# One expert turn with all 128 tokens of the busiest expert, its partner in a half turn, and pairs read from a table

## The chip, the cores and the metric

The kernel runs on one core of a Trainium2 chip. A core has a matmul engine (TensorE, PE in the profile, with its weight loads as PEld), a vector engine (VectorE, DVE), a scalar engine (ScalarE, ACT), GpSimd (POOL) and a sync engine (SyncE, SP) that issues most of the DMAs here. The metric is the device time of one execution in microseconds, as the median of three runs.

## The reference, cut to what matters

The program is one transformer block over 256 tokens of width 1024 with a mixture of experts in it, followed by two further layers. Only the mixture of experts is changed. Each token picks 4 of 32 experts, and each expert is two matrix products with a gated activation between them:

```
def moe_ffn(h, router_w, router_b, w1, b1, w2, b2):
    ...
    logits = (xt @ router_w + router_b).astype(jnp.float32)
    top_v, top_e = lax.top_k(logits, TOP_K)          # TOP_K = 4 of 32
    gate = jax.nn.softmax(top_v, axis=-1)
    ...
    def expert_block(args):
        rows, e = args
        xb = xt[rows]
        hb = xb @ w1[e] + b1[e]                       # 1024 -> 2048
        g, u = hb[:, :D_EXPERT], hb[:, D_EXPERT:]
        g = jnp.minimum(g, SWIGLU_LIMIT)
        u = jnp.clip(u, -SWIGLU_LIMIT, SWIGLU_LIMIT)
        glu = g * jax.nn.sigmoid(g * SWIGLU_ALPHA)
        return ((u + 1.0) * glu) @ w2[e] + b2[e]      # 1024 -> 1024
    ...
    out = jnp.zeros((N, D), y.dtype).at[row_tok].add(y * row_w[:, None].astype(y.dtype))
```

The weights of one expert are 1024 x 2048 and 1024 x 1024 in fp32, 12 MB together, and all 32 experts are used. With the reference's inputs its router sends 69 tokens to expert 9, 63 to expert 6 and fewer to every other; expert 8, the other one of expert 9's pair, gets 27.

## The kernel before

The mixture of experts is a row of 17 turns, named in `MOE_TURNS` (L123): pair 0, then "over", then pairs 1 to 15. A pair turn does experts 2q and 2q+1 together. Each expert has CAP = 64 token places, and the two experts lie side by side on the two 64-column strips of the PE array. The "over" turn is for the one expert that has more than 64 tokens. It takes that expert's tokens 64 to 127, and both strips work on the same 64 tokens: one strip multiplies the even 128-row chunks of the weights and the other the odd ones (`rows_gemm` L1861, `c.over`). `turn_rows` L1883 then adds the two strips by a matmul with `twin`, which folds them, where a pair turn has a transpose. The weights of that expert are so loaded twice, once in its own pair turn and once in the "over" turn.

A turn has three parts, gate, up and down. In each, a pair turn uses 8 slots, a slot being 128 x 2048 fp32 (1 MB, two 128-row chunks of one expert's weights). The "over" turn uses 4 slots in each part. For a pair turn a slot costs 4 matmuls of 128x64 by 512 columns, and so does a slot of the "over" turn. Each matmul stands twice in the trace, since fp32 takes two passes, so 32 records are 16 matmuls.

The order on PE in a turn is (`experts` L1860): the first half of the gate part, the result of the turn before (L1911, 16 records; after the "over" turn ahead of it the biases, L1925), the second half of gate, the selection transposed (L1900), a piece of another network (`ctx_products(0)`, L1956, from turn 2 on), the first half of up, the gate transposed (L1892, or L1890 with `twin` in the "over" turn), the second half of up, half of the gather of the next turn's tokens (L1849), the transposed up part, the other half of the gather, `ctx_products(1)`, and the down part. Turns 0 and 1 have no context pieces, but two `mod` slots each (L2206 on DVE). In turns 13 to 16 the context piece is another one (L1967).

All these weights stream through a ring of 10 places: places 0 to 8 and the buffer hT (`MOE_RING` L120). SP walks one list (`stream` L926): for each transfer it waits until PE has released the place's holder of 10 transfers before, and issues the next. Which expert is the busiest is found at run time by DVE (`find_busiest` L2656), which leaves its number in `route_ints` and then posts `count_ready`; SP and DVE read it into a register (`busiest_expert` L918, TENSOR_LOAD L921) for the "over" turn. Addresses of all other turns are constants. If an expert other than the busiest has more than 64 tokens, or the busiest more than 128, a further loop of rounds runs; here it does not.

Of the kernel before, what the change touches and what calls it, by code (L numbers as in the profile page):

```python
# [63 lines left out]
COLS_E = N_EXPERTS + 2  # L64
# [58 lines left out]
MOE_TURNS = [0, "over"] + list(range(1, PAIRS))  # L123
MOE_COLUMNS = [PAIRS * 2 if pair == "over" else 2 * pair for pair in MOE_TURNS]
# [24 lines left out]
class Plan:  # L149
# [59 lines left out]
    def moe_slot(self, n, pair, j):  # L209

        name, e, at = MOE_SLOTS[j]
        self.moe_slots[n, j] = s = len(self.stream)
        self.stream.append((name, pair if pair == "over" else 2 * pair + e, at, 2, 0, D))
        return s
# [6 lines left out]
    def moe_part(self, n, pair, part, kps):  # L221

        for kp in kps:
            for e in range(1 if pair == "over" else 2):
                s = self.moe_slot(n, pair, part * PART_SLOTS + 2 * kp + e)
                if kp < DC // 2 - 1 or (e == 0 and pair != "over"):
                    self.slot_signal(s)
# [324 lines left out]
def build(nc, ins, out):  # L552
    with ExitStack() as ctx:
# [29 lines left out]
        route_ints = sb("route_ints", [P, 4], I32)  # L583
# [88 lines left out]
        place2 = small[:, 512:512 + TB * COLS_E].rearrange("p (b e) -> p b e", b=TB)  # L672
        gate2 = small[:, 580:580 + TB * COLS_E].rearrange("p (b e) -> p b e", b=TB)
        busiest = small[:, 648:648 + N_EXPERTS]
# [113 lines left out]
        def source(entry, busiest=None):  # L788
            name, index, k0, rows, c0, cols = entry
            if name in ("exp_w1", "exp_w2"):  # L790
                return ins[name][busiest if index == "over" else index][k0].rearrange("p (k n) -> p k n", k=2)
# [12 lines left out]
        class First:  # L804
# [3 lines left out]
            def __init__(self, n, busiest=None):  # L808
                pair = MOE_TURNS[n]
                self.n, self.turn, self.over, self.last = n, n, pair == "over", n + 1 == len(MOE_TURNS)  # L810
                self.experts = (busiest, busiest) if self.over else (2 * pair, 2 * pair + 1)
                self.columns_next = None if self.last else MOE_COLUMNS[n + 1]
# [27 lines left out]
        class Later:  # L840

            x, over = "_x", False
# [75 lines left out]
        def busiest_expert(eng):  # L918

            eng.wait_ge(sem("count_ready"), 1)  # L920
            return eng.value_load(route_ints[0:1, 1:2], min_val=0, max_val=N_EXPERTS - 1)  # L921
# [3 lines left out]
        def _(sp):  # L925
            def stream(s0, s1, busiest=None):  # L926
                for s in range(s0, s1):
# [3 lines left out]
                    sp.dma_start(slot_ap(s, entry[3], entry[5]), source(entry, busiest)).then_inc(landed[PLAN.place[s]], 16)  # L931
# [6 lines left out]
            over = MOE_TURNS.index("over")  # L938
            stream(behind, PLAN.moe_slots[over, 0])
# [2224 lines left out]
```

## Time and profile before

| what | value |
|---|---|
| time, median of three runs (lowest, highest) | 2520.53 us (2520.11, 2523.71) |
| the profiled execution's own time | 2523.49 us |
| its span from the first to the last instruction | 2521.4 us |
| PE busy in the span | 2468.8 us (98%) |
| DMA moved | 778.13 MB, mean 309 GB/s |
| the expert weights among it | 396 transfers of 1 MB |

The span lies 2.1 us below the profiled execution's own time. The mixture of experts runs from about 374 us to about 1482 us of the span. The page cuts the span into 40 slices of 63 us, so that it covers slices 7 to 23 and parts of those beside them. The lines of instructions and of waits say where an engine stood idle and what ended that; the timeline gives single stretches with their start.

### The profile page before, as it was taken

How to read it: one execution, taken by the hardware profiler on the slowest of the kernel's cores; microseconds unless marked ns; L12 is line 12 of the kernel's file. 1: busy time of each engine (PE TensorE's matmuls, PEld its weight loads, DVE VectorE, ACT ScalarE, POOL GpSimd, SP SyncE). 2: the span in 40 equal slices, each digit the busy share in tenths (PEclk: the TensorE clock that was granted, in tenths of full speed). 3: DMA queues.
4: the chain of work that ended last, by engine and by line, in shares of the span. 5: the costliest groups of instructions: out<-in, count | busy, mean ns of one | idle time of the engine just before them, and what ended most of it. 6: DMA issues, size and time to landing. Idle time of an engine off the chain costs nothing. (4 is left out here: it accounts for less than half of the span.)

```text
span 2521.4 us, 36563 instructions
## 1 busy us (share of the span) xinstructions
PE 2468.8 (98%) x16110; PEld 1897.8 (75%) x16110; DVE 1170.8 (46%) x1547; ACT 732.2 (29%) x896; POOL 0.4 (0%) x6
## 2 busy tenths in 40 slices
PE   7999999999999999999999999999999999999998
PEld 6898884555555555555555569999899999999998
DVE  6778763211111111111111149976477667777563
ACT  3355331111011111110111033444544344344442
POOL 0000000000000000000000000000000000000000
PEclk9999989999999999999999999999999999999999
DMA  9844568999999999999999967778267757865651
GB/s 394 302 166 151 218 252 356 421 400 417 418 418 418 419 418 418 418 418 417 397 417 400 397 234 268 282 260 275 74 221 287 288 210 287 305 241 210 215 188 51
DMA packets 156801, 778.13 MB, mean 309 GB/s; under 512 B 12353, under 2 KB 38081, under 8 KB 90593
## 3 DMA queue, kind: packets, MB, share of 16 engines
q1 hardware_dynamic: 152304, 768.68, 78.0%
q10 hardware_dynamic: 4336, 7.07, 0.9%
q8 instruction: 129, 2.11, 0.3%
q14 instruction: 32, 0.25, 0.0%
HBM read 774.66 MB, written 1.05 MB: 308 GB/s over the span
## 5 line engine op out<-in xcount | busy, mean ns | idle before, releaser
L1874 PE MATMUL psum<-ring,arena 128*64 128x512 f32 x2864 | 694.8, 597 | 6.4 <-DMA ring<-in_exp_w 3.5
L1874 PEld LDWEIGHTS psum<-ring,arena 128*64 128x64 f32 x2864 | 220.5, 137 | 418.8 <-issue 415.4
L1491 PE MATMUL psum<-h_high,w_low 128*128 128x256 f32 x1728 | 490.0, 284 | 0.0
L1491 PE MATMUL psum<-h_high,w_high 128*128 128x256 f32 x1728 | 484.3, 281 | 1.4 <-ACT h_high L1290 1.2
L1491 PE MATMUL psum<-h_low,w_high 128*128 128x256 f32 x1728 | 483.6, 281 | 0.0
L2847 DVE TENSOR_TENSOR w_low<-ring,w_high 128x2048 fp32r<-128x2048 f32 (+1 forms) x172 | 374.5, 2191 | 204.2 <-ACT w_high L1277 203.5
L1277 ACT ACTIVATE w_high<-ring 128x2048 fp32r<-128x2048 f32 (+1 forms) x172 | 313.7, 1835 | 380.0 <-PE psum L1491 297.6
L1491 PEld LDWEIGHTS psum<-h_high,w_high 128*128 128x128 f32 x1728 | 328.2, 190 | 5.0 <-issue 4.2
L1491 PEld LDWEIGHTS psum<-h_low,w_high 128*128 128x128 f32 x1728 | 324.7, 188 | 0.0
L1491 PEld LDWEIGHTS psum<-h_high,w_low 128*128 128x128 f32 x1728 | 324.6, 188 | 0.0
L1191 ACT ACTIVATE arena<-psum 128x1024 f32<-128x1024 f32 x68 | 56.8, 862 | 557.5 <-PE psum L1874 557.5
L2206 DVE SCALAR_TENSOR_TENSOR ring<-ring,cond_rows 128x1024 f32<-128x1024 f32 x174 | 206.6, 1220 | 15.3 <-ACT cond_rows L1006 14.5
L2771 DVE TENSOR_TENSOR arena<-psum,arena 128x1024 f32<-128x1024 f32 x32 | 39.2, 1225 | 375.9 <-PE psum L1911 375.9
L1491 PE MATMUL psum<-m_low,w_high 128*128 128x256 f32 x704 | 197.2, 280 | 0.0
L1491 PE MATMUL psum<-m_high,w_high 128*128 128x256 f32 x704 | 196.4, 279 | 0.7 <-DVE arena L2884 0.7
L1491 PE MATMUL psum<-m_high,w_low 128*128 128x256 f32 x704 | 196.8, 280 | 0.0
L2741 DVE TENSOR_TENSOR arena<-psum,vecs 128x512 f32<-128x512 f32 x68 | 43.8, 686 | 296.9 <-PE psum L1892 288.0
L1956 PE MATMUL psum<-arena,ring 128*128 128x256 f32 x640 | 141.4, 379 | 0.0
L1874 PE MATMUL psum<-hT,arena 128*64 128x512 f32 x304 | 134.2, 595 | 0.0
L1491 PEld LDWEIGHTS psum<-m_high,w_high 128*128 128x128 f32 x704 | 132.3, 188 | 0.9 <-DVE arena L2884 0.9
L1491 PEld LDWEIGHTS psum<-m_high,w_low 128*128 128x128 f32 x704 | 132.3, 188 | 0.0
L1491 PEld LDWEIGHTS psum<-m_low,w_high 128*128 128x128 f32 x704 | 132.2, 188 | 0.0
(348 smaller groups left out, 2975.5 us busy)
## 6 DMA issues: line engine op xcount, KB each, us to landing
ring<-in_exp_w SPq DMA_DIRECT2D x358, 1024.0 KB, 11.6
ring<-in_ffn_w SPq DMA_DIRECT2D x108, 1024.0 KB, 5.7
ring<-in_mod_w SPq DMA_DIRECT2D x95, 1024.0 KB, 6.8
hT<-in_exp_w SPq DMA_DIRECT2D x38, 1024.0 KB, 11.7
ring<-in_w_in SPq DMA_DIRECT2D x24, 1024.0 KB, 8.5
ring<-in_ffn_w SPq DMA_DIRECT2D x32, 768.0 KB, 4.9
ring<-in_ctx_w SPq DMA_DIRECT2D x20, 1024.0 KB, 11.8
ring<-in_even_w_in SPq DMA_DIRECT2D x12, 1024.0 KB, 8.1
```

Source lines behind the costliest of these rows:

```text
L1191: act.activation(moe_buf(dst)[:, 0:cols], c.unit(name)[:, 0:cols], ACT.Copy, scale=scale).then_inc(c.free(name), 1)
L1277: act.activation(high_ap(m, cols), slot_ap(s, 2, cols), ACT.Copy).then_inc(sem("w_high_ready"), 1)
L1491: return pe.matmul(unit(u0 + j // 4)[:, (j % 4) * T:(j % 4 + 1) * T], w[:, k % 2, j * P:(j + 1) * P], h[:, k, :], start=first, stop=stop, ...
L1874: mm = pe.matmul(u[strip, cols], x[:, k, strip], c.slot(of)[:, row, cols], start=(kp == 0 and (c.over or r == 0)), stop=(kp == DC // 2 - 1 ...
L1956: mm = pe.matmul(u[:, a * T:(a + 1) * T], w[:, k, a, :], ctx_h[:, k, :], start=(k == 0 and a == 0), stop=(k == DC - 1), skip_group_check=True)
L2206: last = dve.scalar_tensor_tensor(to, w[:, j, :], 1.0, cond_rows[:, row, :], ALU.mult, ALU.mult, accum_out=sums)
L2741: last = dve.tensor_tensor(dst[:, :, strip], rows[:, :, strip], wide(bias, CAP), ALU.add)
L2771: dve.tensor_tensor(dst, c.unit(name).rearrange("p (k t) -> p k t", k=4), dst, ALU.add).then_inc(c.free(name), 1)
L2847: dve.tensor_tensor(low_ap(s, cols), slot_ap(s, 2, cols), high_ap(m, cols).bitcast(F32), ALU.subtract).then_inc(sem("w_split"), 1)
```

## The change

The turns become pair 0, "busiest", "partner" and 14 more pair turns, again 17. In "busiest" both strips take the same expert, strip 0 its tokens 0 to 63 and strip 1 its tokens 64 to 127, from the same slots; so a slot there costs 8 matmuls in place of 4. The other expert of that pair, the partner, takes a turn of its own in the way of the old "over" turn, with its even and odd chunks on the two strips. The pairs of the 14 later turns are read from a table of 16 numbers that DVE writes: entry q is q, or 1 where q is the busiest expert's pair. Pair 0 is left out of the search for the busiest expert, since its turn is already under way. The expert of every turn from turn 1 on is now a number in a register, on SP for the addresses, on DVE for the biases and the selection, on ACT for the gates.

```
-MOE_TURNS = [0, "over"] + list(range(1, PAIRS))
-MOE_COLUMNS = [PAIRS * 2 if pair == "over" else 2 * pair for pair in MOE_TURNS]
+MOE_TURNS = [0, "busiest", "partner"] + list(range(2, PAIRS))
+TURN_COLUMNS = {"busiest": N_EXPERTS, "partner": N_EXPERTS + 2}
+BUSIEST_AT, PARTNER_AT, PAIRS_AT = 1, 2, 4
...
-            for e in range(1 if pair == "over" else 2):
+            for e in range(1 if pair in TURN_COLUMNS else 2):
                 s = self.moe_slot(n, pair, part * PART_SLOTS + 2 * kp + e)
...
+        def turn_of(eng, n):
+
+            kind = MOE_TURNS[n]
+            if kind == 0:
+                return 0
+            at, most = {"busiest": (BUSIEST_AT, N_EXPERTS - 1), "partner": (PARTNER_AT, N_EXPERTS - 1)}.get(
+                kind, (PAIRS_AT, PAIRS - 1))
+            at += 0 if kind in TURN_COLUMNS else kind
+            return eng.value_load(route_ints[0:1, at:at + 1], min_val=0, max_val=most)
...
-            stream(behind, PLAN.moe_slots[over, 0])
-            stream(PLAN.moe_slots[over, 0], PLAN.moe_slots[over + 1, 0], busiest_expert(sp))
-            stream(PLAN.moe_slots[over + 1, 0], PLAN.moe_end)
+            stream(behind, PLAN.moe_slots[1, 0], (0, 1))
+            sp.wait_ge(sem("count_ready"), 1)
+            for n in first_turns[1:]:
+                end = PLAN.moe_end if n + 1 == len(MOE_TURNS) else PLAN.moe_slots[n + 1, 0]
+                stream(PLAN.moe_slots[n, 0], end, First(n, turn_of(sp, n)).experts)
...
             for n in first_turns:
-                experts(First(n))
+                pair_next = n + 1 < len(MOE_TURNS) and MOE_TURNS[n + 1] not in TURN_COLUMNS
+                experts(First(n, None, turn_of(act, n + 1) if pair_next else None))
...
-                        slots = [part * PART_SLOTS + 2 * kp + e for e in range(1 if c.over else 2)]
+                        slots = [part * PART_SLOTS + 2 * kp + e for e in range(1 if c.over or c.alone else 2)]
...
-                                    row, of = (e, slots[0]) if c.over else (r, slots[e])
+                                    row, of = (e, slots[0]) if c.over else (r, slots[0 if c.alone else e])
...
+            partner, pairs = small[:, 160:160 + E], small[:, 392:392 + PAIRS]
...
                 link(dve.scalar_tensor_tensor(key, counts, float(E), iota, ALU.mult, ALU.subtract))
+                link(dve.memset(key[:, 0:2], -1e6))
                 link(dve.max(key_top, key))
...
+                of_pair, other_of_pair = [a.rearrange("p (q e) -> p q e", e=2) for a in (busiest, partner)]
+                for e in range(2):
+                    last = dve.tensor_copy(other_of_pair[:, :, e], of_pair[:, :, 1 - e])
+                link(last)
+                link(dve.tensor_tensor(key, partner, iota, ALU.mult))
+                link(dve.tensor_reduce(small[:, 457:458], key, AX_X, ALU.add))
+                link(dve.tensor_copy(route_ints[:, PARTNER_AT:PARTNER_AT + 1], small[:, 457:458]))
+                link(dve.tensor_reduce(pairs, of_pair, AX_X, ALU.add))
+                link(dve.scalar_tensor_tensor(pairs, iota[:, 0:PAIRS], -1.0, pairs, ALU.add, ALU.mult))
+                link(dve.tensor_tensor(pairs, iota[:, 0:PAIRS], pairs, ALU.subtract))
+                link(dve.tensor_copy(route_ints[:, PAIRS_AT:PAIRS_AT + PAIRS], pairs))
                 dve.tensor_copy(route_ints[:, 0:1], small[:, 460:461]).then_inc(sem("count_ready"), 1)
...
+            of = 0
             for n in first_turns:
-                experts(First(n, busiest_expert(dve) if MOE_TURNS[n] == "over" else None), steps)
+                of_next = turn_of(dve, n + 1) if n + 1 < len(MOE_TURNS) else None
+                experts(First(n, of, of_next), steps)
+                of = of_next
```

On PE, in turn 1 of the kernel before, from the result of turn 0 to the first gather (L1911 is that result, L1874 the weight products, L1900 the selection, L1890 the transposed gate with `twin`, L1849 the gather; here a row is matmuls, not records):

```order
L1911 MATMUL psum<-arena 128x256 x8
L1874 MATMUL psum<-ring,arena 64x512 x4
L1874 MATMUL psum<-hT,arena 64x512 x4
L1900 MATMUL psum<-consts,arena 128x128 x2
L1874 MATMUL psum<-ring,arena 64x512 x8
L1890 MATMUL psum<-arena 128x128 x8
L1874 MATMUL psum<-ring,arena 64x512 x8
L1849 MATMUL psum<-arena 128x128 x8
```

The same place in the changed kernel (its lines stand 15 further down; L1907 is the plain transposed gate):

```order
L1926 MATMUL psum<-arena 128x256 x8
L1889 MATMUL psum<-ring,arena 64x512 x8
L1889 MATMUL psum<-hT,arena 64x512 x8
L1915 MATMUL psum<-consts,arena 128x128 x2
L1889 MATMUL psum<-ring,arena 64x512 x16
L1907 MATMUL psum<-consts,arena 128x128 x8
L1889 MATMUL psum<-ring,arena 64x512 x16
L1864 MATMUL psum<-arena 128x128 x8
```

Between the same neighbours each part of turn 1 has twice the products, on the same number of slots.

On SP, the issues of turn 2 and the start of turn 3 in the kernel before (in_ctx_w are the context's weights):

```order
L931 DMA ring<-in_exp_w 128x2048 x8
L931 DMA ring<-in_ctx_w 128x2048
L931 DMA hT<-in_exp_w 128x2048
L931 DMA ring<-in_exp_w 128x2048 x7
L931 DMA ring<-in_ctx_w 128x2048
```

The end of turn 2 and the start of turn 3 in the changed kernel (TENSOR_LOAD reads the turn's number from `route_ints`, ISA rows are register arithmetic):

```order
L944 ISA
L944 DMA ring<-in_exp_w 128x2048
L934 TENSOR_LOAD route_ints
L934 ISA x2
L944 ISA
L944 DMA ring<-in_exp_w 128x2048
L944 ISA
L944 DMA ring<-in_exp_w 128x2048
```

A load now stands ahead of each turn's first transfer, and a register instruction ahead of each expert transfer.

On DVE, the end of the search for the busiest expert in the kernel before; the last row posts `count_ready`:

```order
L2663 TENSOR_REDUCE small<-small 128x1
L2664 TENSOR_TENSOR small<-small,consts 128x32
L2665 TENSOR_REDUCE small<-small 128x1
L2666 CAST route_ints<-small 128x1
L2667 CAST route_ints<-small 128x1
```

The same place in the changed kernel, from the first of the two casts to the last:

```order
L2684 CAST route_ints<-small 128x1
L2687 COPY small<-small 128x16 x2
L2689 TENSOR_TENSOR small<-small,consts 128x32
L2690 TENSOR_REDUCE small<-small 128x1
L2691 CAST route_ints<-small 128x1
L2692 TENSOR_REDUCE small<-small 128x16
L2693 SCALAR_TENSOR_TENSOR small<-consts,small 128x16
L2694 TENSOR_TENSOR small<-consts,small 128x16
L2695 CAST route_ints<-small 128x16
L2696 CAST route_ints<-small 128x1
```

Nine small instructions stand between the two casts, and a memset (L2676) ahead of them.

## Rows read from the trace of the kernel before

**Rows 1.** The page's 40 slices of the span: granted clock in tenths, and GB/s

```profile
PEclk9999989999999999999999999999999999999999
GB/s 394 302 166 151 218 252 356 421 400 417 418 418 418 419 418 418 418 418 417 397 417 400 397 234 268 282 260 275 74 221 287 288 210 287 305 241 210 215 188 51
```

**Rows 2.** Waits of PE, 300 to 1500 us: total us, times, longest

```profile
PE psum L1892 <- ACT arena L1191: 5.7, 2, 4.5
PE psum L1874 <- DMA ring<-in_exp_w: 3.5, 2, 3.0
```

**Rows 3.** Timeline of ACT: start, us; a turn's finished gate part taken from PSUM

```profile
562.11 1.30 ACT L1191 ACTIVATE arena<-psum 128x1024 f32<-128x1024 f32 x2 [16.42 <-PE psum L1874]
627.42 1.30 ACT L1191 ACTIVATE arena<-psum 128x1024 f32<-128x1024 f32 x2 [16.42 <-PE psum L1874]
...
1285.66 1.30 ACT L1191 ACTIVATE arena<-psum 128x1024 f32<-128x1024 f32 x2 [16.42 <-PE psum L1874]
...
1356.15 1.30 ACT L1191 ACTIVATE arena<-psum 128x1024 f32<-128x1024 f32 x2 [16.42 <-PE psum L1874]
```

**Rows 4.** Windows: us, then busy of the engines; last granted clock, DMA share, GB/s

```profile
420.00:444.00 24.00, 23.48 (x108) 9.48 (x104) 4.04 (x6) 1.11 (x2) 0.00 (x0) 1.00 1.01 422
448.00:450.00 2.00, 2.00 (x6) 0.53 (x4) 1.97 (x5) 0.00 (x0) 0.00 (x0) 0.50 1.03 430
484.00:486.00 2.00, 2.00 (x5) 1.17 (x5) 0.00 (x0) 0.00 (x0) 0.00 (x0) 0.50 1.03 430
562.00:627.00 65.00, 65.00 (x324) 33.83 (x322) 8.89 (x13) 7.22 (x13) 0.00 (x0) 1.00 1.01 418
1285.00:1356.00 71.00, 71.00 (x350) 38.42 (x346) 8.05 (x11) 7.23 (x13) 0.00 (x0) 1.00 0.98 398
```

**Rows 5.** Timeline of PE, turns 1 and 2: start, us, [idle before <- what ended it]

```profile
434.93 1.94 PE L1874 MATMUL psum<-ring,arena 128*64 128x512 f32 x8 [0.52 <-DMA ring<-in_exp_w]
436.79 3.72 PE L1911 MATMUL psum<-arena 128*128 128x256 f32 x16
...
447.45 6.50 PE L1874 MATMUL psum<-ring,arena 128*64 128x512 f32 x16 [2.98 <-DMA ring<-in_exp_w]
453.88 2.05 PE L1890 MATMUL psum<-arena 128*128 128x128 f32 x16
455.86 3.65 PE L1874 MATMUL psum<-ring,arena 128*64 128x512 f32 x16
...
463.12 1.95 PE L1849 MATMUL psum<-arena 128*128 128x128 f32 x16
466.82 5.37 PE L1874 MATMUL psum<-ring,arena 128*64 128x512 f32 x24 [1.75 <-issue]
...
484.70 5.01 PE L1911 MATMUL psum<-arena 128*128 128x256 f32 x16
...
496.94 7.07 PE L1956 MATMUL psum<-arena,ring 128*128 128x256 f32 x32
```

**Rows 6.** Timeline of PEld in turn 1, a weight load that waited for a slot

```profile
450.04 0.27 PEld L1874 LDWEIGHTS psum<-ring,arena 128*64 128x64 f32 x2 [0.59 <-DMA ring<-in_exp_w]
```

**Rows 7.** SP by source line (ns min/median/max), its waits in turns 3 on, DMA landing

```profile
L921 SPq TENSOR_LOAD <-route_ints x1: 471/471/471, 412.4 to 412.4; - x1
...
L931 SPq FUSED_REGOPS  x12: 37/37/48, 413.2 to 444.1; - x12
...
SPq L931 <- PE psum L1956: 164.5, 19, 10.7
...
ring<-in_exp_w SPq DMA_DIRECT2D x358, 1024.0 KB, 11.6
```

**Rows 8.** Timeline around the search: DVE's last casts, its next work, PE's first product

```profile
367.29 0.15 DVE L2667 CAST route_ints<-small 128x1 int32<-128x1 f32 x1
...
373.71 0.49 DVE L2686 TENSOR_TENSOR arena<-consts,small 128x128 f32<-128x128 f32 x2 [3.97 <-ACT arena L1185]
...
373.73 13.95 PE L1874 MATMUL psum<-ring,arena 128*64 128x512 f32 x64 [1.11 <-ACT arena L1185]
```

More of the change, by code:

```diff
@@ L212, in moe_slot @@
         self.moe_slots[n, j] = s = len(self.stream)
-        self.stream.append((name, pair if pair == "over" else 2 * pair + e, at, 2, 0, D))
+        self.stream.append((name, (n, e), at, 2, 0, D))
         return s
@@ L223, in moe_part @@
         for kp in kps:
-            for e in range(1 if pair == "over" else 2):
+            for e in range(1 if pair in TURN_COLUMNS else 2):
                 s = self.moe_slot(n, pair, part * PART_SLOTS + 2 * kp + e)
-                if kp < DC // 2 - 1 or (e == 0 and pair != "over"):
+                if kp < DC // 2 - 1 or (e == 0 and pair not in TURN_COLUMNS):
                     self.slot_signal(s)
@@ L806, in build, with __init__ @@
             x = ""
[L808 to L812, printed above, removed]
+            def __init__(self, n, of=None, of_next=None):
+                kind = MOE_TURNS[n]
+                self.n, self.turn, self.last = n, n, n + 1 == len(MOE_TURNS)
+                self.alone, self.over = kind == "busiest", kind == "partner"
+                self.experts, self.columns_next = None, None
+                if of is not None:
+                    self.experts = (of, of) if kind in TURN_COLUMNS else (of * 2, of * 2 + 1)
+                if not self.last and MOE_TURNS[n + 1] in TURN_COLUMNS:
+                    self.columns_next = TURN_COLUMNS[MOE_TURNS[n + 1]]
+                elif of_next is not None:
+                    self.columns_next = of_next * 2
                 self.gathers = n
@@ L840, in build @@
         class Later:
-            x, over = "_x", False
+            x, over, alone = "_x", False, False
             def __init__(self, r, i, last):
@@ L916, in many, with stream @@
             return eng.value_load(route_ints[0:1, 0:1], min_val=0, max_val=T)
-        def busiest_expert(eng):
-            eng.wait_ge(sem("count_ready"), 1)
-            return eng.value_load(route_ints[0:1, 1:2], min_val=0, max_val=N_EXPERTS - 1)
+        def turn_of(eng, n):
+            kind = MOE_TURNS[n]
+            if kind == 0:
[4 more added lines that the diff above has]
+            return eng.value_load(route_ints[0:1, at:at + 1], min_val=0, max_val=most)
         @block.sync
         def _(sp):
-            def stream(s0, s1, busiest=None):
+            def stream(s0, s1, experts=None):
                 for s in range(s0, s1):
@@ L1876, in rows_gemm @@
                                                    stop=(kp == DC // 2 - 1 and (c.over or r == 1)), skip_group_check=True)
-                                    if half == 1 and row == 1:
+                                    if half == 1 and row == 1 and (e == 1 or not c.alone):
                                         if kp == DC // 2 - 1 and e == 1:
@@ L2665, in find_busiest @@
                 link(dve.tensor_reduce(small[:, 462:463], key, AX_X, ALU.add))
-                link(dve.tensor_copy(route_ints[:, 1:2], small[:, 462:463]))
-                dve.tensor_copy(route_ints[:, 0:1], small[:, 460:461]).then_inc(sem("count_ready"), 1)
-                both = busiest[:, None, :].broadcast_to([P, TB, E])
-                for of in (place2, gate2):
-                    link(dve.tensor_tensor(tmp2, both, of[:, :, 0:E], ALU.mult))
-                    link(dve.tensor_reduce(of[:, :, E], tmp2, AX_X, ALU.add))
@@ new lines, in find_busiest @@
+                link(dve.tensor_copy(route_ints[:, PAIRS_AT:PAIRS_AT + PAIRS], pairs))
+                dve.tensor_copy(route_ints[:, 0:1], small[:, 460:461]).then_inc(sem("count_ready"), 1)
+                for one, at in ((busiest, E), (partner, E + 2)):
+                    both = one[:, None, :].broadcast_to([P, TB, E])
+                    for of in (place2, gate2):
+                        link(dve.tensor_tensor(tmp2, both, of[:, :, 0:E], ALU.mult))
+                        link(dve.tensor_reduce(of[:, :, at], tmp2, AX_X, ALU.add))
+                        link(dve.tensor_copy(of[:, :, at + 1], of[:, :, at]))
```

27 lines of the change are left out of this document (13 added, 14 removed).

## The prediction

> **What bounds the kernel now.** I read the slices first: over the mixture of experts the DMAs move 397 to 421 GB/s and the clock is near full all along [rows 1]. So both the weight stream and PE are candidates, and the question decides the case, because the change leaves out one loading of an expert (12 transfers of 1 MB) and leaves PE's products as they are. The waits of PE come next. Over 300 to 1500 us PE stood idle for expert weights 3.5 us in all, in two pieces [rows 2]; the 5.7 us for ACT lie in turn 0 for the greater part, which the change leaves alone. Then the length of a pair turn: 65.31 us (562.11 to 627.42) with the first context piece, 70.49 us (1285.66 to 1356.15) with the second, longer one [rows 3]. In the first kind of turn 26 transfers of 1024 KB are 27.26 MB in 65.31 us, 417 GB/s, as the window says (418); in the longer turn the rate falls to 398 while PE is busy for all of it [rows 4]. A stream that bounded the turn would hold its rate. With 422 GB/s shown where PE waited on it, the stream needs 64.6 us for 27.26 MB, 0.7 us less than the turn takes. So the pair turns are bounded by PE, with the DMAs close behind.
>
> The Trainium skill, in Trainium Kernel Development and Optimization, section Performance Expectations, calls matmul busy time a poor measure of the distance to the limit, since matmuls are pipelined. That speaks against reading anything from PE's 98%, and nothing here is read from it.
>
> The only place where the stream comes last is turn 1, the "over" turn. It spends 4 matmuls on a slot, 1.8 to 1.9 us (8 records), and pauses only for transposes, while a slot needs 1.049 MB / 422 GB/s = 2.49 us to arrive. The ring runs empty. PE waits 0.52 us for the second gate slot, 2.98 us for the first up slot, and once more inside the next 16 records, where a weight load of the second up slot waits for its DMA [rows 5, 6]. These 16 records take 6.50 us where 16 equal ones soon after take 3.65, and the clock there is at 0.50, 1.2 of 2.4 GHz, after the 2.98 us of idling [rows 4, 5].
>
> **The change part by part.** PE: the products of turns 0 to 2 were full, half, full and become full, full, half. The folding transposes, the biases and the two context pieces occur as often as before. Sum: 0.
>
> Stream: turn 1 still takes 12 expert slots and 2 mod slots, in the same ring places, but now spends 8 matmuls on a slot, about 3.6 us for 16 records [rows 5], against the 2.49 us that a slot needs to arrive. The second gate slot lands at 434.93. PE had done with the first at 434.41 and, with 3.6 us a slot in place of 1.8, now does so at about 436.2. The first up slot lands at 447.45 and was wanted at 444.47; the gate part before it grows by 4 x 1.8 us less the 0.52, so it is wanted at about 451. The second lands at 450.04 and is wanted at about 454.7. So each arrives 1 to 4 us early, the slack grows by 1.1 us a slot, and all three waits go: 0.52 + 2.98 + (6.50 - 3.65) = **6.35 us**. What is late next? After the transposed up part, PE fills in a gather and then waits for DVE's hidden part: from 463.12 to 466.82, 1.75 us idle [rows 5]. Turn 1 still has no context piece there, so that stays as it is. Turn 2, now the half turn, has two context pieces to spread its 12 slots, about 14.7 MB (35 us of stream), over some 43 us of PE: 65.31 less the 96 records that it has fewer, at 3.65 for 16. It starts with a full ring. The turns after it are the pair turns of before, where PE waited for no slot with a poorer start [rows 2]. So the stream gives nothing further back and takes nothing.
>
> The slow clock after the biases (a result of 5.01 us in place of 3.72 [rows 5], clock 0.50 [rows 4]) moves with the half turn from turn 2 to turn 3. I keep it; if it vanished, 1.29 us more would be won.
>
> SP: each turn from 1 on begins with a register load, 0.47 us, and each expert transfer has a register instruction of 0.037 us [rows 7], 24 of them 0.9 us in a turn. The kernel before does both in its "over" turn. I cost them at nothing: SP waits for releases most of a turn, the longest wait on a context piece being 10.7 us, and by the ring's order it comes right behind a turn's first transfer, so right behind the load. A transfer lands 11.6 us after its issue, which at 2.49 us each is some four others ahead of it [rows 7]; a delay of half a microsecond in the issue is lost in that queue. Without the cover it costs what rival 3 says.
>
> ACT and DVE: a load a turn, and a register instruction by each bias, selection and gate operation. The load took 0.47 us on SP [rows 7], and I take it to be the same here. Both stand in front of waits that dwarf it: ACT idles 16.42 us ahead of the gate's eviction [rows 3]. DVE's bias steps lie in the chain to the hidden part, some 0.1 us longer, hidden by a 7 us context piece [rows 5] in all turns but 0 and 1. So 0 to 0.2 us in all; I take 0.
>
> The search: ten small DVE instructions ahead of `count_ready`, each like the cast at 0.15 us and somewhat over with its link, 2 to 2.5 us. `count_ready` moves from about 367.5 to about 370; PE's first product starts at 373.73, when ACT has the gathered tokens, which doesn't depend on it [rows 8]. The rest of the table work (about 1.5 us) delays DVE's next selection from 373.7 to about 375; ACT wants that only after turn 0's gate part, 14 us later [rows 8]. Cost 0. If that cover were gone the whole would be 4 us, once.
>
> Behind the mixture the ring is entered at another place, since 12 transfers are gone. The first two transfers of the next network may go out some microseconds earlier; that network starts from a chain of sums and norms, not from them. I take 0, bounds 0 and -1 us.
>
> Sum: -6.35 us. The profiled execution's 2523.49 becomes 2517.1; the median of the runs lies 3.0 us below that execution, and the same step from it gives 2520.53 - 6.35 = **2514.2 us**.
>
> **The rivals.** (1) The stream bounds after all. Then the 12 transfers count in full, 12.58 MB / 418 GB/s = 30.1 us: 2490.4 us. For it: the DMA share of 1.01 in every pair turn. Against: no wait of PE on a slot after turn 1, and the lower rate in the longer turns [rows 2, 4]. The Trainium skill, DMA: Bandwidth & Descriptors, section Specifications, gives about 358 GB/s as what HBM serves to one core and 435 GB/s as the fabric's ceiling. By the first, as an estimate, a pair turn would be 76 us of stream and this rival would hold; the trace's 418 to 422 GB/s disagrees with it and lies under the second, by which a turn's stream would be an estimated 62.7 us.
>
> (2) The wait moves and takes the clock with it: the idle stretch before turn 1's down part, or a slot that still comes late, drops PE to 1.2 GHz for one stretch as at 448 us. That costs the 2.85 us of that stretch: 2520.53 - 6.35 + 2.85 = 2517.0 us, no change by the bound below. For it: idling of 2.98 us was followed by the low level. Against: the same 1.75 us of idling before down is followed by 24 records in 5.37 us, full speed [rows 5].
>
> (3) Slower: SP's own work. If each of the 14 later pair turns showed its whole load and register work, 0.47 + 0.9 = 1.4 us, as a hole in the stream, and PE ran into that hole, the cost is 14 x 1.4 = 19 us: 2533 us. It decides from 6.35 / 14 = 0.45 us a turn on. For it: the stream has only 0.7 us of room in a turn, and the instructions are in every turn. Against: the depth of the queue, above.
>
> (4) It doesn't do what it says: if the busiest expert were in pair 0, or another had over 64 tokens, the rounds would run, 16 further pair turns of 65 us and more. The reference's counts (expert 9 with 69, the next 63) exclude that but for rounding.
>
> (5) The clock stays up after the biases: 7.6 us won, 2512.9 us.
>
> **How the numbers follow.** Forecast 0.66, rival (1) 0.04, (2) 0.16, (3) 0.07, (4) 0.01, (5) 0.06. About 0.2%, 5 us, is what a measurement of this kernel can tell from no change. The forecast lies only 1.3 us beyond that, and the three runs of before spread over 3.6 us, so about a seventh of it falls within. Faster: 0.57 + 0.04 + 0.06, about 0.66; within 0.26; slower 0.08. The range takes in the forecast, (2) and (5), with about 2 us of spread: 2510.5 to 2519.5 us.
>
> **What would show it.** Right: no wait of PE on an expert slot in turn 1 and none later; a full clock from 420 us on until the biases, now in turn 3; the first context piece of turn 3 some 6.4 us earlier than before; pair turns still 65.3 and 70.5 us, with the DMA rate at 418 and 398; 12 fewer expert transfers. Wrong: pair turns shorter than 65 us (then the stream bounded, rival 1), pair turns longer, with PE waiting for slots near a turn's start (rival 3), or a new stretch at half clock in turns 1 to 3 (rival 2).

## The result

The changed kernel takes 2526.02 us (median of 12 runs, 2520.83 to 2528.15) against 2520.88 us of the kernel before on the same chip (12 runs, 2515.11 to 2523.71): a ratio of 1.0020 with a 95% interval of 1.0011 to 1.0029. It is 5.1 us slower where 6.3 us less were forecast, and lies above the predicted range. The execution that was profiled took 2525.25 us, with a span of 2523.4 us.

| us of the span, one profiled execution each | before | changed | difference |
|---|---|---|---|
| first expert product | 373.73 | 370.51 | -3.22 |
| from there to the last result of the mixture | 1104.53 | 1099.09 | -5.44 |
| from there to the first product of the next network | 21.04 | 27.24 | +6.20 |
| from there to the end | 1022.1 | 1026.6 | +4.5 |

In this pair of executions the mixture so gained nearly what was forecast (the means of all traces, further down, say 4.0 us). The loss is behind it, in code that the change doesn't touch. The four rows add up to 2.0 us and not 5.1: the first one is spread from execution to execution, as the last table shows. In the changed kernel PE's lines stand 15 further on, ACT's 14: L1889 was L1874, L1579 was L1564 (the products that keep the clock up), L1506 was L1491 (the products of the later networks).

PE's waits of the changed kernel from 300 to 1500 us (total us, times, longest), beside [rows 2]:

```profile
PE psum L1907 <- ACT arena L1205: 5.7, 2, 4.5
PE psum L1579 <- issue: 4.3, 1, 4.3
...
PE psum L1889 <- DMA ring<-in_exp_w: 1.2, 1, 1.2
```

The wait for expert weights fell from 3.5 to 1.2 us, and what is left lies ahead of turn 1, in the down part of turn 0. The second row is new: 4.3 us in one piece that the profile ties to nothing. ACT's timeline, a turn's finished gate part, beside [rows 3]:

```profile
553.45 1.30 ACT L1205 ACTIVATE arena<-psum 128x1024 f32<-128x1024 f32 x2 [21.78 <-PE psum L1889]
618.76 1.30 ACT L1205 ACTIVATE arena<-psum 128x1024 f32<-128x1024 f32 x2 [16.42 <-PE psum L1889]
...
1277.00 1.30 ACT L1205 ACTIVATE arena<-psum 128x1024 f32<-128x1024 f32 x2 [16.42 <-PE psum L1889]
...
1347.48 1.30 ACT L1205 ACTIVATE arena<-psum 128x1024 f32<-128x1024 f32 x2 [16.42 <-PE psum L1889]
```

Each row comes 8.66 us earlier (the last 8.67) than its fellow in [rows 3], at the start of the pair turns as at their end, and the turns are as long as they were, 65.31 and 70.48 us. Windows of the changed kernel (busy times of the engines; granted clock, DMA share and GB/s last), beside [rows 4]:

```profile
448.00:450.00 2.00, 2.00 (x12) 0.83 (x12) 1.97 (x5) 1.79 (x5) 0.00 (x0) 1.00 1.05 426
619.00:684.00 65.00, 65.00 (x322) 33.56 (x321) 8.99 (x13) 6.98 (x13) 0.00 (x0) 1.00 1.01 418
1277.00:1347.00 70.00, 70.00 (x346) 38.28 (x345) 8.05 (x11) 7.22 (x13) 0.00 (x0) 1.00 0.98 398
1476.00:1481.00 5.00, 0.73 (x2) 0.43 (x3) 2.90 (x2) 4.98 (x4) 0.00 (x0) 0.56 0.53 215
1481.00:1485.00 4.00, 4.00 (x10) 3.19 (x11) 1.59 (x1) 0.10 (x1) 0.00 (x0) 0.50 0.02 4
```

Turn 1 has the full clock now, and the DMA rates are the old ones, 418 and 398 GB/s. The last two rows are the place of the loss: PE all but idle, and then at half clock.

**The first loss: a pause behind the mixture.** Timelines of PE around the second norm, in the kernel before and in the changed one (start, us, idle before and what ended it):

```profile
1478.26 3.72 PE L1911 MATMUL psum<-arena 128*128 128x256 f32 x16 [1.15 <-ACT arena L1191]
1484.59 3.39 PE L1564 MATMUL psum<-consts 128*128 128x256 f32 x8 [2.60 <-PEq L1569]
...
1494.72 4.05 PE L1564 MATMUL psum<-consts 128*128 128x256 f32 x18
```

```profile
1469.60 3.72 PE L1926 MATMUL psum<-arena 128*128 128x256 f32 x16 [1.15 <-ACT arena L1205]
1476.01 0.48 PE L1579 MATMUL psum<-consts 128*128 128x256 f32 x1 [2.70 <-PEq L1584]
1480.75 3.36 PE L1579 MATMUL psum<-consts 128*128 128x256 f32 x7 [4.26 <-issue]
1483.90 1.06 PE L1600 MATMUL psum<-hT,consts 128*128 128x256 f32 x2
...
1492.26 4.05 PE L1579 MATMUL psum<-consts 128*128 128x256 f32 x18
```

Ahead of this place PE jumps over the rounds that don't run. The waits of 2.60 and 2.70 us are not for another engine: the profile ties them to PE's own queue (L1569, L1584), to PE's first semaphore step behind the jump, and the jump's own record lasts from the first records of the last result until just ahead of that step (ns, start in us; before and changed):

```profile
L2010 PEldq COMPARE_BRANCH  x1: 6087/6087/6087, 1478.3 to 1478.3; - x1
L2025 PEldq COMPARE_BRANCH  x1: 6178/6178/6178, 1469.7 to 1469.7; - x1
```

This standstill is in both kernels. What differs comes behind it. Before, eight products of L1564 run in a row. Now one runs, PE stands for 4.26 us, and seven follow. The norm's products then take 1.06 us a pair at the 0.50 clock (1.2 of 2.4 GHz) until about 1487 us, where they take 0.59 at full clock. From the last result to the first product of the next network that makes 6.20 us. What moves there is visible in the DMA queues: the packets of q8, taken here for the queue that brings PE's program, are 16 KB each (130 of them are 2.13 MB on the page). From 1470 to 1490 us, queue, packets, MB and share of the 16 engines, before and changed:

```profile
q8 instruction: 2, 0.03, 0.7%
```

```profile
q8 instruction: 3, 0.05, 1.1%
```

In the changed kernel they move at 1473, 1478 and 1482 us: the first at the jump, the second right inside the pause, 2.4 us before PE goes on. In the kernel before they move at 1482, again at the jump, and at 1488 us.

**The second loss: slower products with no wait.** From the next network to the end PE waits hardly at all in either kernel, and the clock is full. Windows of the same lengths, before and changed, with the number of products in brackets; the first and the last lie in the second half of a feed-forward network (called out products below), the middle one in a first half:

```profile
1645.00:1685.00 40.00, 40.00 (x346) 40.00 (x345) 30.26 (x30) 14.04 (x8) 0.00 (x0) 1.00 0.79 287
1850.00:1950.00 100.00, 100.00 (x843) 100.00 (x842) 70.46 (x71) 43.25 (x30) 0.00 (x0) 1.00 0.75 269
2460.00:2500.00 40.00, 40.00 (x346) 40.00 (x345) 13.76 (x6) 10.86 (x6) 0.00 (x0) 1.00 0.15 54
```

```profile
1645.00:1685.00 40.00, 40.00 (x335) 40.00 (x335) 28.90 (x28) 12.38 (x7) 0.00 (x0) 1.00 0.73 262
1850.00:1950.00 100.00, 100.00 (x852) 100.00 (x851) 71.73 (x71) 44.22 (x31) 0.00 (x0) 1.00 0.77 274
2460.00:2500.00 40.00, 40.00 (x335) 40.00 (x335) 13.76 (x6) 11.39 (x6) 0.00 (x0) 1.00 0.17 54
```

In 40 us of the out products PE does 335 and not 346. Over 200 starts in a row a product takes 120.0 ns and not 116.7. The products of the first halves are a little quicker (852 against 843 in 100 us). PE's instructions there are the same in kind and order. But one line of the diff, which was not shown ahead of the prediction, moves their data:

```diff
-        route_ints = sb("route_ints", [P, 4], I32)
+        route_ints = sb("route_ints", [P, PAIRS_AT + PAIRS], I32)
         ARENA = 19456
         arena_at = -(-nc.sbuf_base // 32) * 32
         arena = sb("arena", [P, ARENA])
```

The table makes `route_ints` 80 bytes wide in place of 16, and the arena, in which the later networks keep the tokens that stream through PE, begins at byte 151008 of a partition in place of 150944.

### The profile page after: what moved, and what is told of

The parts are those of the page before. It is cut to its first block and busy times, and to the rows that moved or that the text cites. A ratio compares the mean times of both kernels' runs of the same rounds, so it can differ in the third digit from the quotient of the medians.

```text
span 2523.4 us, 37526 instructions
## 1 busy us (share of the span) xinstructions
PE 2469.2 (98%) x16110; PEld 1900.6 (75%) x16110; DVE 1174.7 (47%) x1563; ACT 732.7 (29%) x896; POOL 0.4 (0%) x6
## 3 DMA queue, kind: packets, MB, share of 16 engines
q8 instruction: 130, 2.13, 0.3%
## 5 line engine op out<-in xcount | busy, mean ns | idle before, releaser
L1889 PE MATMUL psum<-ring,arena 128*64 128x512 f32 x2864 | 688.3, 594 | 4.1 <-issue 1.8
L1889 PEld LDWEIGHTS psum<-ring,arena 128*64 128x64 f32 x2864 | 219.3, 137 | 413.3 <-issue 411.9
L1506 PE MATMUL psum<-h_low,w_high 128*128 128x256 f32 x1728 | 486.7, 283 | 0.0
L1506 PE MATMUL psum<-h_high,w_high 128*128 128x256 f32 x1728 | 485.3, 281 | 1.2 <-ACT h_high L1305 1.2
L1506 PE MATMUL psum<-h_high,w_low 128*128 128x256 f32 x1728 | 483.1, 280 | 0.0
L1506 PEld LDWEIGHTS psum<-h_high,w_high 128*128 128x128 f32 x1728 | 324.1, 188 | 4.6 <-issue 3.0
L1506 PEld LDWEIGHTS psum<-h_high,w_low 128*128 128x128 f32 x1728 | 327.2, 189 | 0.0
L1506 PEld LDWEIGHTS psum<-h_low,w_high 128*128 128x128 f32 x1728 | 323.6, 188 | 0.0
L1506 PE MATMUL psum<-m_high,w_high 128*128 128x256 f32 x704 | 199.0, 283 | 0.5 <-DVE arena L2916 0.5
L1506 PE MATMUL psum<-m_low,w_high 128*128 128x256 f32 x704 | 198.6, 282 | 0.0
L1506 PE MATMUL psum<-m_high,w_low 128*128 128x256 f32 x704 | 198.2, 281 | 0.0
L1971 PE MATMUL psum<-arena,ring 128*128 128x256 f32 x608 | 134.4, 379 | 0.0
L1506 PEld LDWEIGHTS psum<-m_high,w_low 128*128 128x128 f32 x704 | 132.9, 189 | 0.0
L1506 PEld LDWEIGHTS psum<-m_high,w_high 128*128 128x128 f32 x704 | 132.3, 188 | 0.7 <-DVE arena L2916 0.7
L1506 PEld LDWEIGHTS psum<-m_low,w_high 128*128 128x128 f32 x704 | 132.4, 188 | 0.0
L1889 PE MATMUL psum<-hT,arena 128*64 128x512 f32 x304 | 130.2, 594 | 0.0
```

The costliest lines, as they stand in the source:

```text
L1506: return pe.matmul(unit(u0 + j // 4)[:, (j % 4) * T:(j % 4 + 1) * T], w[:, k % 2, j * P:(j + 1) * P], h[:, k, :], start=first, stop=stop, ...
L1889: mm = pe.matmul(u[strip, cols], x[:, k, strip], c.slot(of)[:, row, cols], start=(kp == 0 and (c.over or r == 0)), stop=(kp == DC // 2 - 1 ...
L1971: mm = pe.matmul(u[:, a * T:(a + 1) * T], w[:, k, a, :], ctx_h[:, k, :], start=(k == 0 and a == 0), stop=(k == DC - 1), skip_group_check=True)
```

## The experiments

Two theories came out of this: P, the pause hangs on where the jump lands in a 16 KB packet of PE's program (the changed kernel has 11 PE instructions fewer ahead of it, 581 semaphore instructions in its trace against 592); and A, the rate hangs on the first byte of the arena. Their rivals were T (the next network's weights, whose transfers start from other places of the ring, cause the pause) and C (the rate hangs on where the code stands). All times are medians beside runs of the kernel before on the same chip, which differs from group to group. The ratio beside them is estimated from all runs and isn't the quotient of the two medians: it differs from that by up to 0.0006, 1.5 us.

**32 instructions that never run.** They stand in the skipped rounds, behind the jump, and move all that follows by 2 KB (two of these waits make one instruction).

```diff
                 for q in range(4):
                     pe.wait_ge(free_x[q], 1 + ROUND_USES[q] * (ROUNDS - 1))
+                for _ in range(64):
+                    pe.wait_ge(sem("x_ready"), 2)
```

> The changed kernel with 32 more TensorE instructions inside the skipped rounds, behind the jump, so none of them is ever executed: everything behind the mixture stands 32 instructions (2 KB) further on in TensorE's program. Theory P (the 4.26 us in which TensorE waits for nothing at the second norm is the fetch of its next 16 KB instruction packet, because the jump over the rounds lands near the end of one): the pause goes, and with it the half clock behind it, 4.26 + 1.9 = 6.2 us, so 2526.0 - 6.2 = 2519.8 us; the out products of the first feed-forward stay at 120.0 ns each. Theory T (the pause comes from the feed-forward weights, whose transfers start earlier in the changed kernel): the pause stays, 2526.0 us. Theory C (the slower feed-forward products also hang on where the code stands): the pause goes and the 120.0 ns change too.

Measured: 2521.46 us against 2519.83, ratio 1.0004 (0.9995 to 1.0014), by the two ratios some 4 us below the changed kernel where 6.2 were expected. The pause is gone, PE's timeline:

```profile
1475.67 3.54 PE L1579 MATMUL psum<-consts 128*128 128x256 f32 x8 [2.81 <-PEq L1584]
1479.04 0.59 PE L1600 MATMUL psum<-hT,consts 128*128 128x256 f32 x2
```

The last result to the next network takes 21.39 us, 5.85 less. The out products stay at 120.0 ns. That speaks for P, against T and against C.

**The same in the kernel before, the other way.** 488 of these waits, 244 instructions, put its jump where the changed kernel's lands.

> The kernel before with 244 more TensorE instructions inside the skipped rounds, behind the jump: 244 is one 256-instruction packet less the 12 instructions that put the landing of the jump where the changed kernel has it, near a packet's end. Theory P (instruction packet): a pause of about 4 us appears in the kernel before at the second norm, TensorE's clock halves behind it, 2520.9 + 6.2 = 2527.1 us; the out products of the first feed-forward stay at 116.7 ns. Theory T (feed-forward weights): no pause, 2520.9 us. Theory C: the 116.7 ns change too.

Measured: 2526.45 us against 2519.83, ratio 1.0027 (1.0016 to 1.0037). The kernel before now has the pause:

```profile
1479.50 0.79 PE L1564 MATMUL psum<-consts 128*128 128x256 f32 x1 [2.72 <-PEq L1569]
1485.26 3.15 PE L1564 MATMUL psum<-consts 128*128 128x256 f32 x7 [4.97 <-issue]
1488.20 1.06 PE L1585 MATMUL psum<-hT,consts 128*128 128x256 f32 x2
```

27.24 us lie between result and next network, as in the changed kernel, and the out products stay at 116.7 ns. Here no transfer was touched, so T is out.

**Only the width of the table, in the kernel before.**

```diff
-        route_ints = sb("route_ints", [P, 4], I32)
+        route_ints = sb("route_ints", [P, 20], I32)
```

> The kernel before with route_ints 20 columns wide instead of 4 and nothing else: TensorE's program stays the same, the arena begins 64 bytes further on, as in the changed kernel. Theory A (byte of the arena): the out products of the first feed-forward take 120.0 ns and not 116.7, 2520.9 + 4.5 = 2525.4 us, no pause at the second norm. Theory C (code position): 116.7 ns stay, 2520.9 us.

Measured: 2523.15 us against 2519.83, ratio 1.0014 (1.0003 to 1.0024). With PE's program unchanged, the counts in the windows are nearly those of the changed kernel:

```profile
1645.00:1685.00 40.00, 40.00 (x336) 40.00 (x335) 25.65 (x28) 12.56 (x10) 0.00 (x0) 1.00 0.68 238
2460.00:2500.00 40.00, 40.00 (x336) 40.00 (x335) 11.46 (x5) 9.59 (x5) 0.00 (x0) 1.00 0.07 27
```

From the next network to the end it takes 1027.1 us where the kernel before took 1022.1. That is A, and against C.

**The changed kernel with the arena back.**

```diff
-        route_ints = sb("route_ints", [P, PAIRS_AT + PAIRS], I32)
+        route_pad = sb("route_pad", [P, 4], I32)
         ARENA = 19456
         arena_at = -(-nc.sbuf_base // 32) * 32
         arena = sb("arena", [P, ARENA])
+        route_ints = sb("route_ints", [P, PAIRS_AT + PAIRS], I32)
```

> The changed kernel with route_ints placed behind the arena, so that the arena begins at the byte where it does in the kernel before (64 bytes lower than in the changed kernel). Theory A (the products of the feed-forward stages run slower or faster with the byte at which their moving operand in the arena begins): the out products of the first feed-forward take 116.7 ns each again and not 120.0, the 4.5 us lost between the first feed-forward and the end come back, 2526.0 - 4.5 = 2521.5 us, while the 4.26 us pause at the second norm stays. Theory C (the product rate hangs on where the code stands): 120.0 ns stay, 2526.0 us.

Measured: 2521.15 us against 2519.83, ratio 0.9999 (0.9990 to 1.0007). The out products take 116.7 ns, the last stretch 1021.0 us, and the pause stays, 3.95 us:

```profile
1645.00:1685.00 40.00, 40.00 (x345) 40.00 (x344) 30.24 (x30) 13.44 (x7) 0.00 (x0) 1.00 0.76 278
```

```profile
1482.53 3.35 PE L1580 MATMUL psum<-consts 128*128 128x256 f32 x7 [3.95 <-issue]
```

**Both mended.** The last two edits of the changed kernel together, the arena back and the 32 instructions.

> Both mendings in the changed kernel: the 32 never executed TensorE instructions, and route_ints behind the arena. If the two losses are separate (a pause for an instruction packet, and a product rate that goes with the arena's first byte), their gains add: 2526.0 - (2526.0 - 2521.5) - (2526.0 - 2521.2) = 2516.7 us against 2519.8 of the kernel before, no pause at the second norm and 116.7 ns for the out products of the first feed-forward. What is left against the kernel before is then the change itself, 3 to 4 us from the two single-expert turns. Rival: the two are one effect in two guises, and together they give no more than either, 2521 us.

Measured: 2514.35 us (6 runs) against 2520.95, ratio 0.9968 (0.9957 to 0.9980). The gains add, and are if anything larger. Without the two losses the change is worth 6.6 us by the medians and 8.1 by the ratio, with bounds of 5.0 and 10.8: the forecast's 6.35 lies within. There is no pause. One expectation failed: the out products of the first network take 117.8 ns in the profiled execution (the slowest of the six) and not 116.7, with the arena at the same byte:

```profile
1645.00:1685.00 40.00, 40.00 (x342) 40.00 (x342) 29.00 (x29) 12.78 (x8) 0.00 (x0) 1.00 0.73 260
```

**Constants in place of the table.** As the last, with experts and pairs written into the program for these inputs; the table is computed and read by nobody.

```diff
-            return eng.value_load(route_ints[0:1, at:at + 1], min_val=0, max_val=most)
+            return {"busiest": 9, "partner": 8, 4: 1}.get(kind, kind)
```

> The kernel with both mendings, with the numbers of expert, partner and pairs written into the program for these inputs (9, 8, and pair 1 in place of 4) in place of the loads from the table on SP, ACT and DVE; the table is still computed. If the loads lie beside other work, as the prediction had it, the time is that of the kernel with both mendings, within 1 us, and the pair turns take the same 65.3 us. Rival (the loads hold up SP and so the weights): 17 loads and their address arithmetic are 17 x 0.9 = 15 us of SP, and 3 us or more are gained.

Measured: 2513.83 us against 2520.95, ratio 0.9970 (0.9958 to 0.9982). 0.5 us from the last, within the spread of either, and its gate parts at 553.21 and 618.52 us stand 65.31 us apart, as with the loads. So the loads on SP, ACT and DVE cost nothing that can be measured; by the two intervals, 3 us or so could hide in the whole, but not in the pair turns.

**Two more places for the arena.** As the kernel with both mended, `route_pad` with 12 and with 28 columns: first byte 150976 and 151040.

> As the kernel with both mendings, with the arena 32 bytes further on (first byte 150976, a multiple of 64; the two kernels so far stood 32 bytes past one). Theory A64 (the moving operand's rows straddle one more 64-byte piece where they begin at an odd multiple of 32): the feed-forward products fall towards the shortest steps that the traces have shown, 110 ns, 2516.7 us less up to 8000 x 8 ns = 64 us. Theory A0 (the kernels before and changed already differ by 64 bytes at 116.7 and 120.0 ns, so what counts is something else than the place within 64 bytes): between 116.7 and 120.0 ns, 2516 to 2522 us.

> As the kernel with both mendings, with the arena 96 bytes further on (first byte 151040, a multiple of 128). Theory A64: the same rates and time as with 32 bytes. Theory A128 (what counts is the place within 128 bytes): another rate than with 32 bytes. Theory A0: between 116.7 and 120.0 ns, 2516 to 2522 us.

Measured: 2511.83 us (5 runs) with 32 bytes more, ratio 0.9959 (0.9946 to 0.9972), and 2527.29 us with 96 bytes more, ratio 1.0019 (1.0009 to 1.0029). Windows of the first and of the second:

```profile
1850.00:1950.00 100.00, 100.00 (x851) 100.00 (x851) 71.33 (x68) 42.13 (x30) 0.00 (x0) 1.00 0.78 278
2460.00:2500.00 40.00, 40.00 (x342) 40.00 (x341) 12.42 (x11) 9.14 (x7) 0.00 (x0) 1.00 0.02 8
```

```profile
1850.00:1950.00 100.00, 100.00 (x851) 100.00 (x851) 71.78 (x70) 42.51 (x29) 0.00 (x0) 1.00 0.80 283
2460.00:2500.00 40.00, 40.00 (x336) 40.00 (x335) 11.47 (x5) 9.59 (x5) 0.00 (x0) 1.00 0.08 27
```

The last stretch takes 1018.5 and 1029.3 us. Theory A64 falls twice: no stage goes towards 110 ns a product, and two places that are both multiples of 64 differ by 11 us. Both times lie outside A0's 2516 to 2522 us, one on each side. A128 isn't excluded, as the four places are four different ones within 128 bytes. The time goes with the byte; by what rule, the four places don't say.

**The better place for the kernel before.** `route_ints` 12 columns wide, nothing else.

> The kernel before with route_ints 12 columns wide instead of 4 and nothing else: the turns of before, the arena at byte 150976, where the fastest kernel so far has it. Theory A (the byte of the arena sets the rate of the later products, whatever the turns do): from the first feed-forward to the end 1018.5 us as in that kernel and not the 1021 to 1022 of the kernel before, so 2520.9 - 3 = 2518 us; what is then left to the 2511.8 us of the kernel with the new turns, 6 us, is the change itself. Rival (the 32 bytes pay only together with the new turns): 2520.9 us.

Measured: 2515.38 us against 2518.92, ratio 0.9988 (0.9978 to 0.9999), last stretch 1018.2 us. So some 3.5 of the 9.1 us that the fastest kernel gains (0.3 to 5.5 by the interval) belong to the place of the arena and are to be had without the change.

**The jump with some room.** 416 waits, 208 instructions, in the changed kernel.

> The changed kernel with 208 never executed TensorE instructions behind the jump: the jump now lands with some 55 instructions left in the 16 KB packet, against some 8 in the changed kernel and some 230 with 32 instructions. Theory P1 (the next packet is asked for soon after the landing and needs some 4 to 5 us; the 55 instructions cover it): no pause, 2521 us as with 32 instructions. Theory P2 (the next packet is asked for only when the one at hand is used up): the pause of about 4 us stays and only moves from the second keep-warm product into the norm's products, 2526 us.

Measured: 2519.73 us against 2518.92, ratio 1.0004 (0.9995 to 1.0013). No pause, and the eight products run in a row:

```profile
1480.14 2.71 PE L1579 MATMUL psum<-consts 128*128 128x256 f32 x8 [2.85 <-PEq L1584]
1482.64 1.06 PE L1600 MATMUL psum<-hT,consts 128*128 128x256 f32 x2
```

The packets of PE's program move at 1477, 1482 and 1487 us, about 5 us apart as in the changed kernel, but the instructions at hand last until the next one is there. In all twelve traces the second packet moves 5.2 to 6.0 us after the one at the jump, whether or not PE is short of instructions. So the next packet is under way in time, P1, and only a landing close to a packet's end shows. The norm's products run at half clock here too (1.06 us a pair), though the pause isn't there.

**All traces together.** The stretches of the twelve kernels, each from one profiled execution, us:

| kernel | first product | mixture | to the next network | from there to the end |
|---|---|---|---|---|
| before | 373.73 | 1104.53 | 21.04 | 1022.1 |
| before, 244 instructions | 371.59 | 1101.47 | 27.24 | 1021.1 |
| before, arena +64 | 370.47 | 1100.74 | 19.68 | 1027.1 |
| before, arena +32 | 368.95 | 1100.63 | 19.69 | 1018.2 |
| changed (arena +64) | 370.51 | 1099.09 | 27.24 | 1026.6 |
| changed, 32 instructions | 371.17 | 1097.97 | 21.39 | 1025.5 |
| changed, 208 instructions | 374.29 | 1099.28 | 21.57 | 1026.7 |
| changed, arena back | 373.92 | 1097.32 | 27.08 | 1021.0 |
| changed, both mended | 374.95 | 1099.42 | 21.54 | 1022.6 |
| the same, constants | 373.25 | 1096.12 | 21.58 | 1021.1 |
| the same, arena +32 | 376.03 | 1097.36 | 21.55 | 1018.5 |
| the same, arena +96 | 371.96 | 1096.07 | 21.48 | 1029.3 |

The third column has two levels and they go with the landing of the jump: 27.1 to 27.2 in the three kernels with the pause, 19.7 to 21.6 in the others. Within the lower one the eight products behind the jump take 1.99 us in the two kernels with 19.7 and 2.68 to 3.68 us, part of it at half clock, in the seven with 21.0 to 21.6; why the clock falls in some and not in others is open. The last column has four levels, one for each place of the arena (the fourth place has one trace only). Within a place the rate of a stage isn't fixed: with the arena at byte 150944 the first network's out products take 116.7 ns in four traces and 117.8 in the fifth. They take 117.8 in both traces at 150976 and 120.0 in all four at 151008. The move carries all that PE, ACT and DVE read and write in the arena, so whether PE's own reading sets the rate was not separated. The mixture takes 1101.8 us on the mean with the old turns (4 traces) and 1097.8 with the new (8). The first product comes at 369 to 376 us whatever the kernel. What sets it was not followed up; it adds to the spread of the runs.

## Why the prediction was wrong

Point by point, by its own steps.

**PE bounds the turns, with the stream close behind: right.** Pair turns of 65.31 and 70.48 us, at 418 and 398 GB/s, with 12 transfers fewer (384 of experts' weights where there were 396). Rival (1), which wanted shorter turns, is out.

**The waits of turn 1 go: right.** The 2.98 and the 0.52 us are gone in all eight traces with the new turns. A wait of 1.1 to 1.2 us is in three of them, but ahead of turn 1, at the last two slots of turn 0's down part (16 of these 48 records are down, 32 the first half of gate):

```profile
426.97 10.52 PE L1889 MATMUL psum<-ring,arena 128*64 128x512 f32 x48 [1.23 <-DMA ring<-in_exp_w]
```

One trace with the old turns (244 instructions) has it too, 0.95 us, so it isn't the change's.

**The term 6.50 - 3.65 = 2.85 us: taken from one execution, and too large.** The half clock behind the 2.98 us wait was in [rows 4, 5]. Of the three other traces with the old turns one has it in part (5.22 us for these 16 records), and in two it is missing, as with the wider table:

```profile
444.22 1.94 PE L1874 MATMUL psum<-ring,arena 128*64 128x512 f32 x8 [2.98 <-DMA ring<-in_exp_w]
446.61 1.94 PE L1874 MATMUL psum<-ring,arena 128*64 128x512 f32 x8 [0.45 <-DMA ring<-in_exp_w]
```

Two times 8 records take 1.94 us each, full speed, and what is to be saved there is the three waits alone, 0.45 + 2.98 + 0.45 = 3.9 us. The mixture's gain is 4.0 us by the means of the traces, 5.44 by the two profiled executions of the result. The timed runs of the kernel with both mended say 6.6, with bounds of 5.0 and 10.8. One trace a kernel is too little to decide between these; that the 2.85 us are not won each time is shown, how often they are is not. That 6.35 and 6.6 lie close is in part luck.

**The slow clock after the biases moves to turn 3: right.** The result there takes 5.41 us, so rival (5) is out, and with the full clock in turn 1 so is rival (2):

```profile
540.95 5.41 PE L1926 MATMUL psum<-arena 128*128 128x256 f32 x16
```

**SP, ACT and DVE at 0, the search at 0: right.** The kernel with constants and the unchanged length of the pair turns show the first; rival (3) is out. No rounds ran, so rival (4) is out as well. For the second, the first product comes 6.4 to 7.9 us after the last gather ahead of it begins, with the old turns as with the new; only the memset stands ahead of that gather, some 0.1 us. On the mean of all traces the new kernels start later (373.3 against 371.2 us), but 1.9 us of that are there before the search begins.

**"Behind the mixture the ring is entered at another place [...] I take 0, bounds 0 and -1 us": this is the step that failed.** It looked at the part behind the mixture through one thing that moves, the ring, and gave it bounds on one side only, with no reason that excluded a loss. Two other things move, and neither is in the sum. PE's program is 11 instructions shorter ahead of a jump: +6 us. The arena begins 64 bytes further on: +4.9 us from the next network to the end (1026.5 on the mean of four traces against 1021.6 of five). With the 4.0 us gained in the mixture that makes some 7 us lost, where the runs show 5.1. The difference is within the spread of single executions: the stretch ahead of the first product alone varies by 7 us.

The Trainium skill bears on the first of these in Runtime: NRT & Kernel Launch, section Instruction fetch mechanics: programs come in 16 KiB blocks of 256 instructions, the prefetch is sequential, and a taken branch out of the blocks at hand has to fetch its target first. The traces agree: packets of 16 KB, one of which moves at the jump, and 2.60 and 2.70 us in which PE stands there in both kernels with no other engine named. How much of these the packet takes was not separated. What cost 4.3 us is the block behind the one that the jump lands in. By that rule a jump in the program is a place to look at whenever instructions ahead of it come or go, and the prediction had no such step.

**The median.** The predicted time was worked out from the median of three runs, 2520.53. Twelve runs gave 2520.88, so nothing was lost there.

## What to carry to other kernels

A change that adds or removes instructions moves all code behind it, and one that widens a small tile moves all tiles behind that. Both can cost as much as a tuned kernel has left to gain, in stages that the diff doesn't name. So before costing the rest of the kernel at nothing, list the jumps that are taken behind the edit and the tiles whose first byte moves, give each a bound on both sides, and pad or place them so that they stay where they were. A term that rests on the clock of one execution should be looked for in a second one before it goes into a sum.

## What the runs showed of the hardware that was not expected

- A taken jump on TensorE came with 2.60 to 2.86 us of standstill in all twelve traces, and a 16 KB packet of the program that moved at it. Where it landed close to the packet's end, it cost 4 to 5 us more (4.26, 4.97 and 3.95 us in the three traces that have it), and about 2 us at half clock behind that. In these three traces one semaphore step, one weight load and one product run between landing and pause; the 8 instructions left of the expectations are a reckoning, not a reading. With 208 instructions of padding, some 55 left by the same reckoning, there was no such pause.
- Products of 128x256 take 116.7 to 120.0 ns each in the out stages, and the first byte of the arena goes with it: 64 bytes further on, 346 products in 40 us became 335, and 336 where PE's program was left as it was. From the next network to the end that is 1018.2 to 1029.3 us over four places 32 bytes apart. The rule is open.
- A register load with its address arithmetic, on SP and DVE in each of 16 turns and on ACT in 14, could not be measured in the time: 2514.35 us with them, 2513.83 without.
